# Splitting weight panels in halves, with a ring of three raw slots and three buffers for high parts

## The reference

```
# first_block, layers i = 0 and 1
x = layer_norm(ALPHA*x + g1*mixer(modulate(x, sh1, sc1)), ln_g[i,0], ln_b[i,0])   # attention, then pooling
x = layer_norm(ALPHA*x + g2*swiglu(modulate(x, sh2, sc2), ffn_w_in[i], ffn_w_out[i]), ln_g[i,1], ln_b[i,1])
# second_block, one layer
h = rms(x); (a_q .. c_qkv, mix_g) = split(h @ w_in)          # 7644 columns
y_a, y_b, y_c = three attentions, each @ its w_branch         # dsa, nsa, dilated
g = sigmoid(mix_g); x = x + (g[0]*y_a + g[1]*y_b + g[2]*y_c) @ w_out
x = x + (silu(rms(x) @ w_gate) * (rms(x) @ w_up)) @ w_ffn_out
```

## Time and profile before

| | us |
|---|---|
| median of 3 runs (1138.65 to 1139.23) | 1139.21 |
| the profiled execution's own time | 1138.57 |
| its span | 1136.8 |
| PE busy | 1094.0 |
| DVE busy | 817.7 |
| ACT busy | 526.0 |
| POOL busy | 103.7 |

### The profile page before, as it was taken

The page is one execution under the profiler, slowest core; times in us unless marked ns, Lnnn a source line. Parts: engine busy times, 40 slices in busy tenths (PEclk is TensorE's granted clock), DMA queues, the critical chain, the costliest instruction groups (busy, mean ns, idle before and its releaser), DMA issues.

```text
span 1136.8 us, 15613 instructions
## 1 busy us (share of the span) xinstructions
PE 1094.0 (96%) x6209; PEld 902.4 (79%) x6209; DVE 817.7 (72%) x1147; ACT 526.0 (46%) x698; POOL 103.7 (9%) x86
## 2 busy tenths in 40 slices
PE   4999999999999999999999999999999999999998
PEld 2876776887888877888888898877877688888887
DVE  2678788699888888988674686678664776666644
ACT  1435236354444332544453466658565535444432
POOL 0000000000000002000000001065556000000000
PEclk9999999999999999999999999999999999999999
DMA  9998663768988876465955556533342445666553
GB/s 340 339 321 209 255 259 112 268 212 279 322 275 309 304 278 231 147 223 163 301 187 203 174 165 193 179 101 127 114 137 102 167 137 160 185 185 186 185 188 108
DMA packets 145018, 236.90 MB, mean 208 GB/s; under 512 B 4901, under 2 KB 86322, under 8 KB 144690
## 3 DMA queue, kind: packets, MB, share of 16 engines
q1 hardware_dynamic: 138128, 221.12, 57.8%
q10 hardware_dynamic: 6818, 14.78, 4.2%
HBM read 229.33 MB, written 6.55 MB: 208 GB/s over the span
## 4 chain that ended last, share of the span: by engine, by line
PE 47%; DVE 7%; ACT 3%; issue 2%; DMA 1%; POOL 1%; SPq 0%; POOLq 0%; DVEq 0%; ACTq 0%
PE bank L680 45%; DVE ring_lo L1897 1%; PE bank L785 1%; ACT w_hi L1471 1%; DMA ring<-in_ffn_w_in 1%; POOL ring_lo L2867 1%; DVE y_tok L2231 0%; DVE small L2233 0%; SPq L2948 0%; DVE y_tok L2227 0%; DVE small L2706 0%; DVE aux L2688 0%; ACT h L1480 0%; DVE aux L2724 0%; DVE aux L2762 0%
## 5 line engine op out<-in xcount | busy, mean ns | idle before, releaser
L1897 DVE TENSOR_TENSOR ring_lo<-ring,w_hi 128x2048 fp32r<-128x2048 f32 (+3 forms) x145 | 325.3, 2244 | 192.2 <-ACT w_hi L1471 191.8
L1471 ACT ACTIVATE w_hi<-ring 128x2048 fp32r<-128x2048 f32 (+3 forms) x144 | 270.6, 1880 | 336.0 <-PE bank L680 313.2
L680 PE MATMUL bank<-h,w_hi 128*128 128x512 f32 (+1 forms) x1152 | 364.6, 380 | 4.7 <-issue 2.1
L680 PE MATMUL bank<-h,ring_lo 128*128 128x256 f32 x1056 | 281.1, 280 | 0.0
L680 PEld LDWEIGHTS bank<-h,w_hi 128*128 128x128 f32 x1152 | 203.7, 188 | 53.2 <-issue 6.8
L680 PE MATMUL bank<-w_hi,h 128*128 128x512 f32 (+4 forms) x640 | 191.7, 383 | 4.0 <-ACT big L1753 2.1
L680 PEld LDWEIGHTS bank<-h,ring_lo 128*128 128x128 f32 x1056 | 193.0, 189 | 0.5 <-issue 0.5
L680 PEld LDWEIGHTS bank<-w_hi,h 128*128 128x128 f32 x640 | 118.5, 188 | 28.3 <-issue 6.7
L680 PE MATMUL bank<-ring_lo,h 128*128 128x512 f32 (+4 forms) x320 | 115.0, 379 | 0.0
L680 PE MATMUL bank<-w_hi,ff_hi 128*128 128x512 f32 x264 | 103.1, 390 | 2.4 <-DVE ring_lo L1897 1.7
L680 PE MATMUL bank<-w_hi,ff_lo 128*128 128x512 f32 x264 | 102.7, 389 | 0.0
(11 more groups left out here) (275 smaller groups left out, 1359.1 us busy)
## 6 DMA issues: line engine op xcount, KB each, us to landing
aux<-in_w_mod SPq DMA_DIRECT2D x24, 2048.0 KB, 9.4
ring<-in_ffn_w_in SPq DMA_DIRECT2D x88, 512.0 KB, 5.0
ring<-in_w_in SPq DMA_DIRECT2D x24, 1024.0 KB, 5.0
ring<-in_ffn_w_out SPq DMA_DIRECT2D x22, 1024.0 KB, 5.1
ring<-in_w_ffn_in SPq DMA_DIRECT2D x44, 512.0 KB, 4.8
ring<-in_attn_w_qkv SPq DMA_DIRECT2D x12, 1024.0 KB, 11.4
ring<-in_w_ffn_out SPq DMA_DIRECT2D x11, 1024.0 KB, 5.0
bias_rows<-srow ACTq DMA_DIRECT2D x1, 5376.0 KB
```

Source lines behind the costliest of these rows:

```text
L680: return nc.tensor.matmul(o, l, r, start=start, stop=stop, **kw)
L1471: nc.scalar.activation(panel_part(i, 0), raw_panel(i), ACT.Copy).then_inc(w_hi, 1)
L1897: V.tensor_tensor(panel_part(i, 1), raw_panel(i), panel_part(i, 0).bitcast(F32), ALU.subtract)\
```

## The change

RING goes from 4 to 3 and PARTS from 2 to 3: one raw slot and one slot for low parts go, one buffer for high parts comes. High and low parts are made in two halves (two chunks each); each half has its own count, and TensorE waits for the first half, runs its chunks over all tiles, and then waits for the second. This holds in `gemm` for nb > 0, in `gemm_by_tile` save the sweeps, the first group and the last one, and in `ffn_block_in_pairs` for kg 0; everywhere else TensorE still waits for the whole panel. The end of the first half is also signalled, and the first half of a later high part may be written then. `halves_before` has its first key at RING, and the gate bias too, so both move from panel 4 to panel 3. In the `ffn`s ACT's silu is moved ahead of the second `split_to` of its block, and DVE's addition for the gate ahead of its products with `w_mod`. The calls of `next_high`, `next_low` and `z_ahead` are not edited. The core of the diff:

```diff
-RING = 4
-PARTS = 2
+RING = 3
+PARTS = 3
@@ waits
-        def wait_hi_free(eng, i):
+        def wait_hi_free(eng, i, half):
 
             if ordinal[i] >= PARTS:
-                eng.wait_ge(*done[split_panels[ordinal[i] - PARTS]])
+                j = split_panels[ordinal[i] - PARTS]
+                if half == 0 and half_columns(i) <= half_columns(j):
+                    eng.wait_ge(*first_half_done.get(j, done[j]))
+                else:
+                    eng.wait_ge(*done[j])
...
-                eng.wait_ge(w_hi, high_parts(i))
+                eng.wait_ge(w_hi, 2 * ordinal[i] - 1 + half)
...
-                eng.wait_ge(w_lo, by_dve[i])
+                eng.wait_ge(w_lo, 2 * by_dve[i] - 1 + half)
@@ TensorE
+            def by_half(key, lo, hi):
+
+                i = panel_at[key]
+                for half in range(2):
+                    wait_hi(pe, i, half)
+                    wait_lo(pe, i, half)
+                    mid = (lo + hi) // 2
+                    yield half, range(mid, hi) if half else range(lo, mid)
+
+            def release_first_half(key, ins):
+
+                ins.then_inc(w_used, 1)
+                released[0] += 1
+                first_half_done[panel_at[key]] = (w_used, released[0])
...
                 for kg in range(2):
-                    w = panel((name + "_in", nb, kg))
+                    w = panel((name + "_in", nb, kg), True, kg == 1)
+                    if kg == 0:
+                        for part, cs_ in by_half((name + "_in", nb, kg), 0, PK):
+                            for lo, key in sides:
+                                if part == 0:
+                                    take(key, PAIR_POOL[name])
+                                ins = chunks(w, key, lo, kg, cs_)
+                            if part == 0:
+                                release_first_half((name + "_in", nb, kg), ins)
+                    else:
+                        for lo, key in sides:
+                            ins = chunks(w, key, lo, kg, range(PK))
+                            fills(ins, key)
@@ ScalarE
-                wait_hi_free(act, i)
                 wait_landed(act, i)
-                if lo_by_pool[i]:
...
-                else:
-                    nc.scalar.activation(panel_part(i, 0), raw_panel(i), ACT.Copy).then_inc(w_hi, 1)
+                for half in range(2):
+                    wait_hi_free(act, i, half)
+                    nc.scalar.activation(half_of(i, 0, half), raw_half(i, half), ACT.Copy).then_inc(w_hi, 1)
...
                         split_to(panel_at[(name + "_in", nb, 0)] + 2)
                         low_halves(name, "g", nb)
+                        gate(name, nb)
                     split_to(last_panel(name + "_in", nb) + 2)
@@ VectorE
-                    wait_hi(dve, i)
-                    V.tensor_tensor(panel_part(i, 1), raw_panel(i), panel_part(i, 0).bitcast(F32), ALU.subtract)\
-                        .then_inc(w_lo, 1)
+                    for half in range(2):
+                        wait_hi(dve, i, half)
+                        V.tensor_tensor(half_of(i, 1, half), raw_half(i, half), half_of(i, 0, half).bitcast(F32),
+                                        ALU.subtract).then_inc(w_lo, 1)
```

More of the change, by code:

```diff
@@ L453, in wait_hi, with wait_lo @@
             else:
[L454 to L460 removed]
+                eng.wait_ge(w_hi, 2 * ordinal[i] - 1 + half)
+        def wait_lo(eng, i, half=1):
             if lo_by_pool[i]:
@@ L664, in fills, with panel @@
                 ins.then_inc(filled[where[key][0]], 1)
-            def panel(key, low=True):
+            def panel(key, low=True, whole=True):
                 i = panel_at[key]
@@ L673, in panel @@
                     return [raw_panel(i)]
+                if not whole:
+                    return [panel_part(i, 0), panel_part(i, 1)]
                 wait_hi(pe, i)
@@ L716, in gemm @@
                 for kg, (lo, hi) in enumerate(groups):
-                    w = panel((stage, nb, kg), nb > 0)
+                    w = panel((stage, nb, kg), False, nb == 0)
                     if nb == 0:
@@ L725, in gemm @@
                     else:
[L726 to L731, removed]
+                        for half, cs_ in by_half((stage, nb, kg), lo, hi):
+                            for tt in tts:
+                                for c in cs_:
+                                    ins = product(banks[tt][:, 0:width], lhs(tt, c), [x[:, c - lo, :] for x in w],
+                                                  c == 0, c == last)
+                                if half and hi - 1 == last:
+                                    fills(ins, (stage, nb, tt))
+                            if half == 0:
+                                release_first_half((stage, nb, kg), ins)
                     release((stage, nb, kg), ins, (stage, nb, tts[-1]) if hi - 1 == last else None)
@@ L741, in gemm_by_tile @@
                         by_sweeps = stage == "w_out" and nb == 0
+                        halved = not (by_sweeps or final or both)
                         if nb == 0 or not both:
-                            w = panel((stage, nb, kg), not by_sweeps)
+                            w = panel((stage, nb, kg), not by_sweeps, not halved)
                         cut = slice(nb * NB, nb * NB + NB) if both else slice(0, NB)
@@ L754, in gemm_by_tile @@
                                         fills(ins, (stage, nb, tt))
-                        for tt in () if by_sweeps else range(TT):
+                        if halved:
+                            for half, cs_ in by_half((stage, nb, kg), lo, hi):
+                                for tt in range(TT):
+                                    if (kg, half) == (0, 0):
+                                        take((stage, nb, tt), pool)
+                                    for c in cs_:
+                                        if nb == 0 and tt == 0:
+                                            for key in inputs(c):
+                                                wait_emptied(pe, key)
+                                        ins = product(psum[where[(stage, nb, tt)][0]], lhs(tt, c),
+                                                      [x[:, c - lo, :] for x in w], c == 0, c == last)
+                                if half == 0:
+                                    release_first_half((stage, nb, kg), ins)
+                        for tt in () if by_sweeps or halved else range(TT):
                             if kg == 0:
@@ L858, in ffn_block_in_pairs @@
             def ffn_block_in_pairs(name, nb):
-                for kg in range(2):
-                    w = panel((name + "_in", nb, kg))
[L862 to L874, removed]
+                sides = [(half * 256 + s * P, (name, side, s, nb)) for half, side in enumerate("gu") for s in range(2)]
@@ new lines, in chunks @@
+                def chunks(w, key, lo, kg, cs_):
+                    bank = psum[where[key][0]]
+                    for c in cs_:
+                        mm(bank[:, :], w[0][:, c, lo:lo + P], h_pair[:, kg * PK + c, :],
+                           kg == 0 and c == 0, False, skip_group_check=True)
+                        ins = mm(bank[:, SEQ:], w[1][:, c, lo:lo + P], hT[0][:, kg * PK + c, :],
+                                 False, kg == 1 and c == PK - 1, skip_group_check=True)
+                    return ins
@@ L1679, in low_halves, with gate @@
                                      ACT.Copy).then_inc(low_copied, 1)
+            def gate(name, nb):
+                wait_emptied(act, (name, "g", 0, nb))
+                if nb >= 2:
+                    wait_emptied(act, ff_key(name, nb - 2))
+                empties(nc.scalar.activation(tmp[:, nb % 2, :], gate_sum, ACT.Silu), (name, "g", 1, nb))
             def ffn(name):
```

31 lines of the change are left out of this document (14 added, 17 removed).

## The result

The changed kernel takes 1180.09 us (median; 1178.01 to 1184.09), the kernel before 1139.06 beside it: a ratio of 1.0365 (95% interval 1.034 to 1.039). It is slower, as forecast, but by 41 us and not by 27, and outside the range of 1151 to 1175. The profiled execution took 1181.28.

The account below looks back on a forecast made before the run. TensorE, busy 1094.0 of 1136.8 us, was taken as the bound. The profiled 1138.57 us plus 23.3 of stalls and 3.4 of clock gave 1165.3, a median of 1166, with an 8-in-10 range of 1151 to 1175.

Parts of the forecast that it names:

- the clock: Whole kernel: new idle stretches of TensorE make its granted clock fall; two falls, +3.4 us (0 to 8.5).
- The stalls: Whole kernel: TensorE's added waits, summed over all places before any clock loss, +23.3 us.
- Steady stretches: ffn2 and most of ffn1: no waits to give back, so they stay as they are, 0.
- ffn0: 240 to 440 us: gains from halved panels cancel against panels landing late behind w_mod loads, 0 (-4 to +4).
- Panel 67: ffn1: bias load issued a beat later delays this panel's landing; wait 5.9 us, before 1.8, +4.1 (0 to +6).
- z: Panel 95's later load delays z_out(4) and the index scores, +5.0 (0 to +6); panel 85's wait goes, -0.2.
- Dense pieces: Calls adding PARTS make ACT wait out a whole load after each piece; +14.4 us together (7 to 20), 2.1 at the beginning.
- kind A: Dense pieces where `next_high` comes ahead of the probabilities' copy: the copy is late for TensorE, +5.7 us.
- ahead of `w_out`: After panels 120 and 121, later low parts delay gating and the turned rows: +2.6 and +4.0 us.
- Only the halves matter: Rival: landings are hidden everywhere, waits for low parts, issue in ffn0 and silu go; faster, 1131 us; chance 0.06.
- Only single places: Rival: only panels 67 and 95 cost, the dense pieces hide their waits; 1150 us; chance 0.12.
- Loads late throughout: Rival: in ffn0 each of five pairs of w_mod loads costs a further 2 to 3 us; 1178 us; chance 0.05.

Follow-up runs that it names:

- the probes: Kernel before with five idle stretches of TensorE put into ffn2, in two sets of lengths: 1165.58 us (1.025) and 1165.52 us (1.0239).
- places: next_two with panel 95's high part moved behind z_out(4) and the index scores, and the bias table loaded in seven pieces: 1150.87 us, 1.012.
- places_two: places with panel 95 split earlier, after the first index-score tile on ACT, and the w_mod load moved behind panel 17: 1137.65 us, 0.9997.
- next_two: Changed kernel with `next_high` and `next_low` asking for the panel + 2 again instead of + PARTS: 1158.19 us, 1.018.
- halves_alone: Changed kernel with RING = 4 and PARTS = 2 again, keeping halved parts and all other edits: 1129.12 us, 0.9927.
- gap_probe: Kernel before with POOL additions making TensorE idle ahead of five ffn2 blocks (stalls of 1.14 to 8.04 us): 1165.58 us, 1.025.

## Why the prediction was wrong

**The step that failed** is the clock: "The change makes five idle stretches of 2.2 to 5.9 us; I count two falls, 3.4 us (0 to five, 8.5)." The mechanism was named, and its size was off by a factor of five: eight stalls of 2.0 to 7.4 us, a fall at each, 18.1 us of busy time. The count was wrong (two falls for eight) and so was the price (1.7 us, from the one of the earlier trace rows, for 2.3). Even the stalls were miscounted: the sum's own terms hold six of 2.2 us and more (5.9 twice, 4.0, 3.0, 2.6 and 2.2), not five. I had taken a fall as something that may or may not come; every stall of 4 us or more brought one, in the traces of all runs. Even the upper end of my own bound, 8.5, left the forecast 9 us short. With 18.1 in place of 3.4 it would have been 1180.7.

In "TensorE: Matmul & The Clock Gate", section on HAM oscillation, the Trainium skill ties the loss to idle gaps beyond a certain length. In these runs the long stalls bear it out (all of 4 us and more), but stalls down to 1.71 us had a fall too. "By it each new gap adds a fall" was my own widening of it. The wide form fits the eight stalls of the changed kernel, and I gave it no chance of its own, but it is no rule either: the stalls of 1.14, 1.69 and 2.23 us in the probes had no fall, and neither had the one of 1.73 us at 767 in the trace of before, which I had at hand.

**The stalls** came to 24.5 us for 23.3, but not term by term, and that the sums are so close is partly luck: behind wo they are 27.4 us, and a gain of 3.6 ahead of it that the forecast did not have brings them down.
- Steady stretches: right. ffn2 is 184.69 for 184.68, so no wait in mid panel shows there.
- The start to the end of wo: 3.6 us of idle time gone that I had not counted, and TensorE came 3.1 us early to the tokens of ffn0. Panel 17 took it back: TensorE waited 4.08 us for it, to 239.17, which is 0.9 us later than in the kernel before (238.25). Forecast: 1.5 late. So what was gained ahead of a landing was waited out at it, with a fall of the clock on top.
- ffn0, 0 forecast (-4 to +4): +4.7 of idle time (2.48 and 2.25), just outside the bound; with the gain ahead of it +1.2. Panels 38 and 48, named as 1.3 us late, were not: TensorE waited 0.4 us at 48 and not at all at 38. Panel 24 was late, which I had not named: issued at 276.7, it landed at 289.8, beside `w_mod` and three row loads of ACT's queue (277.7 to 278.5), which in the kernel before met the panel after it. I had counted SP's loads and left out ACT's. That they are the cause is read from this order alone; no run moves them.
- Panel 67: +5.6 for +4.1 (bound 6). The bias went out at 550.53, the panel landed at 569.8, and the wait was 7.35 us, not 5.9. places shows its cause.
- z: +3.9 for +4.8, with the mechanism as described: high part of panel 95 at 725.58 behind a landing, z_out(4) behind it, and the next banks after that. places and places_two show both sides of it.
- Dense pieces: +2.2 for +2.1 at the beginning; kind A +3.3 for +5.7, since unit 17 had its 3.0 (2.77) but its neighbours 0.5 and 0.6 for 2.2 and 1.0; ahead of `w_out` +7.6 for 6.6. next_two shows that `+ PARTS` is the cause of all of them.

**The rivals.** "Only the halves matter" has the right sign for the halves and would have been the outcome with four slots (1131 forecast, 1129 measured). "Only single places" fell, since dense pieces do not hide their waits. "Loads late throughout" gave 1178, near the time that came, but not with its mechanism: it put 12 us into ffn0, 2 to 3 at each of five pairs of `w_mod` loads. ffn0 did come out 10.1 us longer (4.7 idle, 5.4 busy), which my forecast of 0 had missed, but mostly by two stalls, at panels 17 and 24, and their falls. In part this rival stands: 8 us that places_two still loses there against halves_alone.

Not settled: of the 4.0 us of busy time in the rest of ffn0, the fall behind panel 24 explains 1.7 and the one near 446, which begins inside this stretch here and behind it before, 0.9. The other 1.4 are not clock: the same stretch is 2.3 us busier than before in places_two, at a clock of 1.00, and 0.6 less busy with four slots, so they come with the ring; by what, no run shows. The fall near 446 itself has no wait of more than 0.4 us in the 30 us before it here.

## What to carry to other kernels

Price a new stall of TensorE as idle time plus clock: here stalls of 4 us and more always cost some 2 us on top, and those near 2 us did in some executions and not in others. When a ring gets shorter, look through every place that speaks in panels ahead (here `+ PARTS`), every load in front of or beside the panels on any queue, and every in-order program that puts a wait for a landing ahead of the moves that free banks. Measure the parts of such a change alone: its useful half (halved parts, 8 us) was hidden behind a loss in the other. And compare a repaired kernel with the best one, not only with the one before: places_two is level with the kernel before, and that still hides 8 us.

## What the runs showed of the hardware

- Every stall of TensorE of 4.0 to 8.0 us in the traces of these runs (21 of them, the initial load aside) came with 3.4 to 10.2 us at 1.2 GHz, which began in the stall or within 1 us behind it. Longer stalls had longer ones, but loosely: 8.04 and 7.35 us had 10.2, 6.95 had 6.8, 4.42 had 3.4, and 2.77 had 6.8 as well. Of TensorE's work these stretches cost 2.3 us each in the changed kernel (18.1 for eight).
- Stalls of 1.7 to 2.8 us had such a stretch or had none, the same stall in different executions too (2.50 and 2.49 us at 443, 1.73 and 1.71 at 767). 1.14 and 1.69 us in gap_probe had none.
- Dummy matmuls of 0.22 us in the idle time kept the clock at 2.4 GHz in five of six places; where they could not start during the stall they did not.
- A panel of 1 MB, for which 5.0 us is the median, took 13.1 us beside a 2 MB load and three row loads of another queue (276.7 to 289.8).
